# Two attention stages of a two-model forward pass: the next pair's transposes and scores are put ahead of this pair's weights and values

## What is computed

```
h = h + 0.5 * swiglu(rms_norm(h, norm_ffn1[i]), ffn1_w_gate_up[i], ffn1_w_down[i])
hn = rms_norm(h, norm_mix[i])
kind, j = i % N_MIXERS, i // N_MIXERS
if kind == 0:   mix = stick_breaking_attention(hn, ...)
elif kind == 1: mix = moba_attention(hn, ...)
else:           mix = mla_attention(hn, ...)
h = h + mix
h = h + 0.5 * swiglu(rms_norm(h, norm_ffn2[i]), ffn2_w_gate_up[i], ffn2_w_down[i])
```

```
q, k = partial_rotary(q, pos), partial_rotary(k, pos)
l_own = jnp.einsum('bhqd,bhkd->bhqk', qc, k_own) * scale
p = softmax(where(opos <= cpos, l_own, NEG));  o = p @ v_own;  return from_heads(o) @ w_o
```

```
logits = (einsum(qn, k_nope) + einsum(qr, k_rope)) * scale
p = softmax(where(kpos <= qpos, logits, NEG));  o = p @ v;  return from_heads(o) @ w_o
```

## Time and profile before

| what | value |
|---|---|
| median of 3 runs | 4962.53 us (4962.01 to 4971.61) |
| the profiled execution | 4961.05 us |
| its span, first to last instruction | 4959.3 us |
| PE busy | 82% of the span |
| DVE, ACT, POOL busy | 40%, 31%, 24% |
| mean DMA rate | 131 GB/s |
| mean granted TensorE clock | 0.895 of full |

### The profile page before, as it was taken

How to read it: one execution, slowest core, us unless ns; L and a number is a source line. 1 busy time by engine, 2 the same in 40 slices (tenths; PEclk the granted TensorE clock), 3 DMA queues, 4 the chain that set the end, 5 groups by cost and what they waited for, 6 DMA issues and landing times.

```text
span 4959.3 us, 45454 instructions
## 1 busy us (share of the span) xinstructions
PE 4058.9 (82%) x17223; PEld 3073.9 (62%) x17223; DVE 1996.8 (40%) x2138; ACT 1528.4 (31%) x1898; POOL 1199.2 (24%) x800
## 2 busy tenths in 40 slices
PE   4987979889698887987897976677898977566989
PEld 3854868657586676765676744664386845564467
DVE  3534445325353354535444434213245432324144
ACT  3345424224342343436333311011143421102033
POOL 3610656205563055630450000100000000110000
PEclk9998989999898998999998977888998987778999
DMA  4633646336463265643563411011454522001444
GB/s 149 218 90 107 219 159 229 113 117 210 160 216 112 78 220 174 215 130 91 178 220 107 161 60 61 1 60 61 143 180 144 188 77 78 0 13 47 154 152 144
DMA packets 490210, 649.31 MB, mean 131 GB/s; under 512 B 13051, under 2 KB 390418, under 8 KB 490066
## 3 DMA queue, kind: packets, MB, share of 16 engines
q1 hardware_dynamic: 466832, 568.50, 34.5%
q0 software_dynamic: 20736, 75.51, 4.6%
q10 hardware_dynamic: 2498, 3.39, 0.2%
HBM read 646.29 MB, written 1.05 MB: 131 GB/s over the span
## 4 chain that ended last, share of the span: by engine, by line
issue 57%; POOLq 15%; PE 13%; POOL 8%; DVE 3%; DMA 2%; ACT 1%; DVEq 0%; SPq 0%
POOL lora_w L495 6%; POOLq L510 5%; POOLq L502 5%; POOLq L500 3%; PE bank L701 2%; POOLq L508 2%; PE bank L937 2%; PE bank L1037 1%; PE bank L708 1%; PE bank L710 1%; PE bank L709 1%; PE bank L1044 1%; PE bank L1046 1%; DMA gate<-in_mod_w 1%; DMA wproj<-in_w_in 1%
## 5 line engine op out<-in xcount | busy, mean ns | idle before, releaser
L708 PE MATMUL bank<-wproj_hi,x_lo 128*128 128x512 f32 x2112 | 848.9, 402 | 58.3 <-DVE x_lo L1612 51.2
L710 PE MATMUL bank<-wproj_hi,x_hi 128*128 128x512 f32 x2112 | 832.5, 394 | 0.0
L709 PE MATMUL bank<-wproj_lo,x_hi 128*128 128x512 f32 x2112 | 832.1, 394 | 0.0
L701 PE MATMUL bank<-wproj,xT 128*128 128x384 f32 (+2 forms) x1984 | 769.2, 548 | 23.9 <-DMA wproj<-in_w_in 11.0
L1554 DVE TENSOR_TENSOR wproj_lo<-wproj,wproj_hi 128x4096 fp32r<-128x4096 f32 x132 | 615.9, 4666 | 324.3 <-ACT wproj_hi L1187 324.3
L701 PEld LDWEIGHTS bank<-wproj,xT 128*128 128x128 f32 x1984 | 381.9, 196 | 395.9 <-issue 256.8
L708 PEld LDWEIGHTS bank<-wproj_hi,x_lo 128*128 128x128 f32 x2112 | 403.0, 191 | 151.9 <-DVE x_lo L1612 56.0
L1187 ACT CAST wproj_hi<-wproj 128x4096 fp32r<-128x4096 f32 x132 | 480.1, 3637 | 20.7 <-DMA wproj<-in_ffn_w_gate_up 15.3
L710 PEld LDWEIGHTS bank<-wproj_hi,x_hi 128*128 128x128 f32 x2112 | 402.0, 190 | 87.3
L709 PEld LDWEIGHTS bank<-wproj_lo,x_hi 128*128 128x128 f32 x2112 | 403.5, 191 | 80.1
L471 POOL TENSOR_SCALAR rstd<-sumsq 128x2 f32<-128x2 f32 x21 | 4.0, 191 | 1804.5 <-ACT tok L1182 1766.5
(11 more groups left out here) (359 smaller groups left out, 5184.6 us busy)
## 6 DMA issues: line engine op xcount, KB each, us to landing
wproj<-in_ffn_w_gate_up SPq DMA_DIRECT2D x176, 1024.0 KB, 7.6
wdown<-in_ffn_w_down SPq DMA_DIRECT2D x132, 1024.0 KB, 5.6
wproj<-in_w_in SPq DMA_DIRECT2D x52, 1024.0 KB, 6.2
wproj<-in_ffn_w_gate SPq DMA_DIRECT2D x44, 1024.0 KB, 5.3
wproj<-in_ffn_w_up SPq DMA_DIRECT2D x44, 1024.0 KB, 7.8
gate<-in_mod_w POOLq DMA_DIRECT2D x72, 512.0 KB, 4.0
oT<-in_mod_w POOLq DMA_DIRECT2D x72, 512.0 KB, 5.2
wproj<-in_sb_w_qkv SPq DMA_DIRECT2D x48, 512.0 KB, 5.5
```

Of the source, the lines that this page charges most:

```text
L701: last = nc.tensor.matmul(proj_ps[t][:, 0:rhs.shape[2]], lhsT[:, c, t * P:(t + 1) * P], rhs[:, c, :], start=(c == 0), stop=(c == kc - 1))
L708: nc.tensor.matmul(ps, rounded(a_lo), rounded(b), start=first, stop=False, skip_group_check=True)
L709: nc.tensor.matmul(ps, rounded(a), rounded(b_lo), start=False, stop=False, skip_group_check=True)
L710: return nc.tensor.matmul(ps, rounded(a), rounded(b), start=False, stop=final, skip_group_check=True)
```

## The change

In the steps of moba and mla, PE runs `turn_pair` and `scores` of pair i+1 ahead of `turn_probs` and `values` of pair i, and ACT runs `copy_qk` of pair i+1 ahead of `copy_pt` of pair i. The lists of DVE, POOL and SP are as before. The stick-breaking and the diff stages keep their order on every engine. No instruction is added or removed, and no semaphore or wait is changed.

```
@@ -887,10 +887,10 @@      (PE)
                     if more:
                         project_pair(i.plus(1), w.plus(1), 0)
                         project_pair(i.plus(1), w.plus(1), 1)
-                    if more and kind == "sb":
+                    if more and kind != "diff":
                         next_scores(i.plus(1))
                     weigh_values(i)
-                    if more and kind != "sb":
+                    if more and kind == "diff":
                         next_scores(i.plus(1))
@@ -1287,14 +1287,14 @@    (ACT)
                     if more:
                         evac(i.plus(1), w.plus(1), 0)
                         evac(i.plus(1), w.plus(1), 1)
+                    if more and kind != "diff":
+                        copy_qk(i.plus(1))
                     if kind == "sb":
-                        if more:
-                            copy_qk(i.plus(1))
                         exp_arg(i, u, 0)
                         exp_arg(i, u, 1)
                     copy_pt(i, 0)
                     copy_pt(i, 1)
-                    if more and kind != "sb":
+                    if more and kind == "diff":
                         copy_qk(i.plus(1))
```

## The result

| | before | after |
|---|---|---|
| median | 4962.27 us (4960.6 to 4971.61) | 5021.01 us (5018.89 to 5030.66) |
| ratio after / before, 95% interval | | 1.0125 (1.0112 to 1.0138) |
| the profiled execution, its span | 4961.05, 4959.3 us | 5019.5, 5017.8 us |

The change makes the kernel 58.7 us slower. The prediction said 54.9 us slower (5017), inside a range of 5000 to 5042. On a second chip, whose before kernel runs at 4928.93 us, the ratio was 1.0164 (1.0127 to 1.0202).

The account below looks back on a forecast made before the run. Moba was taken as bound by PE, mla by a ring of 10.26 us. Moba 13.7 + mla 27.9 + clock 13.3 = 54.9 us on 4961.05 gives 5016.0, with 1.5 for the median 5017; range 5000 to 5042.

Parts of the forecast that it names:

- PE waits for `prepare`: Between projection and transposes of q and k, PE idles: 1.62 + 0.06 us in moba, nearly 4 us in mla.
- ring: Mla's period as a loop: `prepare`, transposes, copies, scores, logits, weights, `evac`, `prepare`; 10.26 us before, 14.24 after.
- Moba +1.80 per pair: Moba, projection end to next projection: 6.59 us against 4.79, six times, and +2.88 in the seventh step; +13.7 us.
- `outputs` ahead of the logits put `values` into mla's ring; 14.24 at full clock: Mla: next logits wait on DVE behind `outputs`, hence for `values`; period 14.24 against 10.26, +27.9 us in all.
- The clock, +1.9 per mla pair: TensorE falls to 1.2 GHz in every mla pair: +0.5 on transposes, +1.4 on scores, +13.3 us over seven pairs.
- A: Rival: the clock holds in mla despite the new wait; time 5004, chance 0.13.
- B: Rival: the clock falls in every moba pair as well, 3.3 x 7 = 23 us more; time 5040, chance 0.17.
- C: Rival: faster, next pair's softmax starts at the scores, beside `turn_probs` and `values`; -3 us, time 4960, chance 0.04.
- D: Rival: the new waits are hidden by misread ACT or DVE slack; time stays at 4962, chance 0.03.

Follow-up runs that it names:

- filled_mla: The changed kernel with seven more matmuls that nobody reads in PE's wait between projection and transposes in mla; ratio to before 1.0086.
- after_again: The changed kernel, unchanged, measured again on another chip as the base for the runs beside it; ratio to before 1.0164.
- split: The before kernel with only PE's list altered in moba and mla: `turn_pair` between the two heads' `values`, `scores` after both; ratio to before 0.9988.

## Why the prediction was right

*PE waits for `prepare`.* Right for moba, in place and size: 1.62 + 0.06 us forecast, 1.74 seen, and cutting `prepare` by 0.86 cut the period by as much. For mla the wait of nearly 4 us is that of a ring at full clock: in the pair of `filled_mla` above, the filler of 3.19 and the wait of 0.93 take its place. In the changed kernel itself PE waits 2.3 to 3.4 us, because part of the projection before it runs at the lower clock (its first six MATMUL instructions take 2.15 us instead of 1.19).

*Moba +1.80 per pair.* 17.1 to 17.3 against 15.31 is +1.9. The whole stage, from the first copy of q and k to the output copies behind it, grew by 18.4 us (947.06 to 1084.49, 137.4 us; before, 953.39 to 1072.45, 119.1). At full clock it would be 13.9, against 13.7 forecast: 11.3 in six periods and 3.2 at the end (2.88 forecast), less 0.6 in the first period. The other 4.5 are the clock, which the forecast had at nothing in moba: 2.9 in the one long period, and 1.6 in the last pair. There `turn_probs` and `values` of the seventh pair take 3.66 us from the start of the first to the start of the last group of instructions, where in `after_again` they take 2.28, and the stretch from the last copy of q and k to the output copies is 16.75 us, where `after_again` has 15.12.

*`outputs` ahead of the logits put `values` into mla's ring; 14.24 at full clock.* Right: 14.0 with the wait filled, 12.8 with `outputs` moved behind as well.

*The clock, +1.9 per mla pair.* This term was mis-sized. That it falls in every pair was right, but I let it be back behind the scores, and it stayed low through `turn_probs` and `values`: from the start of the scores to that of `turn_probs` 3.58 us instead of 1.83 (as in `filled_mla`; the 1.62 of the forecast runs from weight load to weight load), from there to the next projection 4.17 instead of 2.45. The transposes, for which I had put 0.5, were slow in only two of seven pairs. The cost was 3.9 per pair in six pairs, which is the upper end that I had given (3.9). The term is 23 us in these six, and 25 with the seventh and measured against the forecast's own ring (52.9 less 27.9), where I had 13.3.

*Why the sum still came out.* By luck: the clock was priced too low, and layers outside the two stages came out shorter. Mla's stage grew by 52.9 us (1616.65 to 1703.01 before, 1617.54 to 1756.83 after) and moba's by 18.4, 71.3 in all, 16.4 above the forecast. Of this 4.5 came back in the output projections behind them. The stretches from the layers' norms to the stages were 4.5 us shorter, and the other layers 3.8 in sum (single feed-forward layers by -8.0 to +3.1). Those layers moved by as much in experiments that do not touch them, so this part is no effect of the order that I could show. Nor did the forecast foresee the 4.5 us of the output projections, as it had everything outside the two stages keep its length. The total was nearer to the forecast than its terms were.

*Rivals.* A (the clock holds in mla) is out by the granted clock of 0.67 there, and `filled_mla` shows what it costs. B (it falls in every moba pair) is out too: one or two of seven do. C is out as it stood; its mechanism is real, though, once DVE's list is altered, and even then the stage is slower than before (12.8 against 10.3). D (the new waits are hidden) is out by the time itself.

## What to carry to other kernels

Moving work forward in one engine's list pays only if its inputs are ready at that point: look for what the later work was covering before you move it out of the way, as `turn_probs` and `values` covered `evac` and `prepare` here. Where the consumer's engine has its own fixed order (`outputs` ahead of the next logits), earlier scores buy nothing and the moved work joins the ring. The same order is right in the stick-breaking stage, where the opposite move cost 1.28%: the softmax is long there and nothing prepares q and k. So the order must be chosen stage by stage. And a wait on PE is to be priced with the slow work after it.

## What was not expected

Seven matmuls of no use in PE's wait made the mla stage some 20 us shorter. And in moba the clock can fall without any long wait: after waits of 0.29 and 0.68 us around small transposes and 64-column products the scores took 2.00 us instead of 1.14, with PE's order as before the change. It fell once in a stick-breaking stage of `split` as well, which no edit touched.
